# The last local-attention pair of an encoder kernel: V turned in one go, splits and Y's lower parts moved, a second weights buffer for the last merge

## The chip, the cores and the metric

One core of a Trainium2 chip runs the whole program. The metric is the time of one execution on the device, in microseconds (us); the kernel before and the changed kernel are compared by the median of several executions.

## The reference, cut to what matters

A two-layer encoder trunk on one sequence of 1,024 tokens by 1,024 features, float32.

```
x = x + even_mixer(rmsnorm(x))     # 8 heads dilated windows (mixer A), 8 heads 2-D neighbourhood (mixer B)
x = x + swiglu(rmsnorm(x))
x = x + odd_mixer(rmsnorm(x))      # differential attention, 8 heads
x = x + swiglu(rmsnorm(x))
out = rmsnorm(x)

# even_mixer
proj = h @ w_in                                       # q, k, v of both mixers
ya = dilated_mixture_attention(qa, ka, va)            # branches weighted by their softmax denominators
yb = neighborhood_attention(qb, kb, vb, rpb)          # each token: 8 x 16 neighbours on a 16 x 64 grid
y = concatenate([ya, yb]) @ w_out
```

## The kernel before, in words

**Pairs.** Attention works on pairs of heads P: 0 to 3 are mixer A, 4 to 7 mixer B ("local"), 8 to 15 the second layer. The change touches the end of mixer B, pair 7, and the output projection behind it (`out_projection(0)`). Each pair has eight steps n, one for 128 queries (for a local pair, a stripe of 8 grid columns), and each step handles both heads m = 0 and 1.

**Precision.** Every product is made of three passes: an operand x is split into a high part (ScalarE rounds it, `ACT.Copy` to fp32r) and a lower part (VectorE subtracts the high part from x). So each tile of weights (`w_split`, WR to WS), each turned tile of probabilities (`hi`, `lo`, to ATB), each block of V (`vhi`, `vlo`, to VS) and each block of the attention output Y (`y_high`, `y_low`, to HH and HL) costs a ScalarE and a VectorE instruction, the second waiting for the first.

**One step of a local pair.** TensorE computes scores (`qk`, L2462) one step ahead; VectorE adds the bias table and takes the minimum (`ttr`, L1760); ScalarE takes the exponential with the row sum (`exp`, L1141); TensorE transposes the probabilities (`turn`, L2501); ScalarE and VectorE make high and lower part (`hi` L1182, `lo` L1835). After each second step TensorE multiplies with V (`pv`, L2545), ScalarE copies one half (`y_copy`, L1231) and VectorE adds the other (`y_add`, L1844).

**The order of the work.** Each engine's program is a list written out by hand (`attention_mixed` once for each engine), with waits on semaphores between engines; each engine works strictly in its list's order. Tables say at which step something is put in: `splits(P)` (weight splits, as step: strip ahead, slot, fills that must be done), `turned_v` (the transposes of V, `tv`, L2395), `Y_AT` and `Y_LOW_AT` (high and lower parts of Y), `Y_ORDER` (the order in which blocks of Y go into the projection). In pairs 4 to 6 the next pair's projection (`fill`, L2381) fills TensorE between the steps. In pair 7 nothing is left to fill with behind step 0, where its own V is finished.

**V in pair 7.** The second half of V is evacuated by VectorE at step 1 (`evac`, L1715). The transposes of V come in two batches of four: the first between the two turns of step 1, the second behind them.

**The output projection.** `op_item(0, i)` multiplies block `Y_ORDER[0][i]` of Y with two strips of `w_out` (12 matmuls of 512 columns). It waits for i + 1 lower parts of Y. Item 0 stands between the two turns of step 7; items 1 and 2 stand behind the last turn, each followed by one of the last two products with V; item 3 and the spread of the row sums follow, then the rest:

```
for m in range(2):
    op_item(0, m + 1)
    pv(7, NQ - 1, m)
op_item(0, 3)
```

**The merge of mixer A.** The three dilated branches are kept as two partial outputs and merged for each pair: MY = MY x weight 0 (`merge_start`), MZ = MZ x weight 1, MY += MZ (`merge_rest`), all on GpSimd, in chunks of 256 columns, four instructions for each. Both weights are broadcast from DRAM into one buffer, MA, so the second weights are fetched only when the first multiplication is done. The result goes to `y_dram` and is loaded back as a block of Y (YE for blocks 0 and 1, Y for the others); `y_scale` multiplies blocks 4 to 6 with their reciprocal row sums on GpSimd. Pair 3's merge runs beside pair 7.

**Transfers.** All loads named here are issued by SyncE in the order of `attention` and `out_projection` in `sync_program`. `raw(w)` loads the two halves of weight strip w into WR, each once the split of the strip before has freed it.

## Time and profile before

| | us |
|---|---|
| median of 3 runs | 2536.59 |
| lowest, highest | 2532.62, 2537.97 |
| the profiled execution's own time | 2532.99 |
| its span (first to last instruction) | 2531.0 |
| mean granted TensorE clock in it | 0.997 of full |
| TensorE busy | 2502.5 |
| VectorE busy | 1758.6 |
| ScalarE busy | 1155.8 |
| GpSimd busy | 413.7 |

The profile records one execution. PE is TensorE, DVE VectorE, ACT ScalarE, POOL GpSimd, SP SyncE. A busy time is the sum over an engine's instructions; in a timeline, an instruction's idle time before it is given in brackets with what ended it. Matmuls are pipelined, so rows overlap; the step between two starts is the time one costs. The granted clock is given as a share of 2.4 GHz. Pair 7 lies from about 470 us to 500 us.

### The profile page before, as it was taken

The numbers are of one execution on the slowest core, as the hardware profiler recorded it, in microseconds if no ns is written. First come the engines' busy times: TensorE is split into PE (matmuls) and PEld (weight loads), VectorE is DVE, ScalarE is ACT, GpSimd is POOL, SyncE is SP. The second block draws the span as 40 slices with busy tenths as digits, with TensorE's granted clock in tenths as the row PEclk, the third lists the DMA queues.
The fourth block names the chain that finished last, engine by engine and source line by source line (L and its number), as shares of the span: only waits on it lengthen the run. The fifth ranks groups of instructions, "written<-read, shape, count | busy, mean of one in ns | idle before, by whom it ended". The sixth has DMA issues, their size and how long they took to land.

```text
span 2531.0 us, 34993 instructions
## 1 busy us (share of the span) xinstructions
PE 2502.5 (99%) x12931; PEld 2065.0 (82%) x12931; DVE 1758.6 (69%) x2647; ACT 1155.8 (46%) x2016; POOL 413.7 (16%) x320
## 2 busy tenths in 40 slices
PE   9999999899999999999999999999999999999998
PEld 7888777688888888888888888888888888888887
DVE  6556565656878878666577777777657878887654
ACT  6555554625333333444455455556343333334434
POOL 1001022400332333100000000000002333232001
PEclk9999999999999999999999999999999999999999
DMA  3222253633444444866211111111334444447764
GB/s 130 61 60 74 53 134 94 186 127 117 147 178 162 146 171 166 316 216 210 80 48 50 50 50 50 48 49 71 117 108 143 168 155 164 156 154 268 237 194 145
DMA packets 189171, 332.38 MB, mean 131 GB/s; under 512 B 59728, under 2 KB 67792, under 8 KB 180816
## 3 DMA queue, kind: packets, MB, share of 16 engines
q1 hardware_dynamic: 154208, 320.62, 37.5%
q10 hardware_dynamic: 34800, 9.60, 1.8%
q8 instruction: 101, 1.65, 0.3%
q14 instruction: 62, 0.51, 0.1%
HBM read 238.24 MB, written 91.91 MB: 130 GB/s over the span
## 4 chain that ended last, share of the span: by engine, by line
PE 93%; issue 2%; DVE 2%; ACT 1%; DMA 1%; SPq 1%; POOL 0%; ACTq 0%; POOLq 0%; DVEq 0%
PE PS L2381 20%; PE PS L2296 18%; PE PS L2297 18%; PE PS L2298 18%; PE PS L2545 4%; PE PS L2477 4%; PE PS L2501 3%; PE PS L2493 1%; PE PS L2448 1%; PE PS L2522 1%; PE PS L2395 1%; PE PS L2462 1%; PE PS L2304 1%; PE PS L2526 1%; PE PS L2438 0%
## 5 line engine op out<-in xcount | busy, mean ns | idle before, releaser
L2381 PE MATMUL PS<-HH,WS 128*128 128x512 f32 x1536 | 515.9, 402 | 3.5 <-DVE HL L1623 1.1
L2381 PEld LDWEIGHTS PS<-HH,WS 128*128 128x128 f32 x1536 | 285.5, 188 | 59.9 <-issue 1.6
L2381 PE MATMUL PS<-HL,WS 128*128 128x512 f32 x768 | 301.4, 393 | 0.0
L2097 DVE TENSOR_TENSOR SPLIT<-RAWI,SPLIT 128x1024 fp32r<-128x1024 f32 x154 | 194.2, 1265 | 149.9 <-ACT SPLIT L1450 149.9
L1450 ACT ACTIVATE SPLIT<-RAWI 128x1024 fp32r<-128x1024 f32 x154 | 162.9, 1060 | 205.7 <-PE PS L2298 152.2
L2296 PE MATMUL PS<-TH,WS 128*128 128x512 f32 x640 | 249.2, 389 | 2.3 <-ACT SIL L1442 2.3
L2298 PE MATMUL PS<-TH,WS 128*128 128x512 f32 x640 | 249.0, 389 | 0.0
L2297 PE MATMUL PS<-TL,WS 128*128 128x512 f32 x640 | 249.0, 389 | 0.0
L2296 PE MATMUL PS<-SPLIT 128*128 128x512 f32 x616 | 240.2, 390 | 0.0
L2298 PE MATMUL PS<-SPLIT 128*128 128x512 f32 x616 | 239.7, 389 | 0.0
L2297 PE MATMUL PS<-SPLIT 128*128 128x512 f32 x616 | 239.7, 389 | 0.0
L2296 PE MATMUL PS<-FH,WS 128*128 128x512 f32 x608 | 236.9, 390 | 0.0
L2298 PE MATMUL PS<-FH,WS 128*128 128x512 f32 x608 | 236.6, 389 | 0.0
L2297 PE MATMUL PS<-FL,WS 128*128 128x512 f32 x608 | 236.5, 389 | 0.0
L1424 ACT ACTIVATE WS<-WR 128x512 fp32r<-128x512 f32 x136 | 85.1, 629 | 242.0 <-PE PS L2298 116.6
L1760 DVE CUSTOM_DVE_ANT_0 PS<-PS,BIASC 128x1024 f32<-128x1024 f32 x128 | 154.2, 1246 | 24.4 <-PE PS L2477 23.3
L2381 PEld LDWEIGHTS PS<-HL,WS 128*128 128x128 f32 x768 | 145.0, 189 | 25.2
L2041 DVE TENSOR_TENSOR WS<-WR,WS 128x512 fp32r<-128x512 f32 x136 | 118.3, 871 | 61.1 <-ACT WS L1424 61.1
L2041 DVE TENSOR_TENSOR WS<-UR,WS 128x512 fp32r<-128x512 f32 x120 | 106.0, 884 | 71.5 <-ACT WS L1424 71.3
L1424 ACT ACTIVATE WS<-UR 128x512 fp32r<-128x512 f32 x120 | 75.8, 632 | 153.5 <-PE PS L2298 113.7
L2296 PEld LDWEIGHTS PS<-TH,WS 128*128 128x128 f32 x640 | 120.1, 188 | 28.1 <-ACT SIL L1442 3.2
L1145 ACT ACTIVATE EC<-PS,ST 128x1024 f32<-128x1024 f32 x128 | 141.2, 1114 | 3.8 <-DVE ST L1760 3.8
(274 smaller groups left out, 4969.8 us busy)
## 6 DMA issues: line engine op xcount, KB each, us to landing
WR<-wstrips SPq DMA_DIRECT2D x224, 256.0 KB, 2.7
RAWI<-ab_scratch SPq DMA_DIRECT2D x154, 256.0 KB, 4.2
ab_scratch<-SIL SPq DMA_DIRECT2D x132, 256.0 KB, 2.0
WD<-wdown SPq DMA_DIRECT2D x22, 1024.0 KB, 7.5
wd_scratch<-WD SPq DMA_DIRECT2D x22, 1024.0 KB, 3.9
RAWI<-wd_scratch SPq DMA_DIRECT2D x88, 256.0 KB, 3.3
UR<-wstrips SPq DMA_DIRECT2D x80, 256.0 KB, 3.3
RAWI<-wdown SPq DMA_DIRECT2D x66, 256.0 KB, 3.8
```

Source lines behind the costliest of these rows:

```text
L1145: e.activation(e_tile(kind, m, n)[:, 0:128 * nk], banks(S_BANK[m], 2)[:, 0:128 * nk], ACT.Exp, scale=-1.0, bias=ST[:, n % 2, m:m + 1], acc ...
L1424: e.activation(WS[:, slot, 0, :], src, ACT.Copy).then_inc(S["w_hi"], 1)
L1450: e.activation(SPLIT[m % 6][:, 0], RAWI[:, m % 4], ACT.Copy).then_inc(S["ihi"], 1)
L1760: e.tensor_tensor_reduce(out=s, in0=s, in1=(table if kind == "C" else table[:, m, :])[:, c:c + 128 * nk], scale=-1.0 if kind == "B" else 1 ...
L2041: e.tensor_tensor(WS[:, slot, 1, :], src, f(WS[:, slot, 0, :]), ALU.subtract).then_inc(S["w_lo"], 1)
L2097: e.tensor_tensor(SPLIT[m % 6][:, 1], RAWI[:, m % 4], f(SPLIT[m % 6][:, 0]), ALU.subtract).then_inc(S["ilo"], 1)
L2296: e.matmul(ps, wh, xh, start=start, stop=False, skip_group_check=on)
L2297: e.matmul(ps, wh, xl, start=False, stop=False, skip_group_check=on)
L2298: return e.matmul(ps, wl, xh, start=False, stop=stop, skip_group_check=on)
L2381: last = e.matmul(ps, wt, xt, start=g == 0, stop=g == 23)
L2477: last = e.matmul(PS[:, S_BANK[m] + c // 4, 0:wd], QS[r, a, q], KS[r, P % 2, b, k], start=i == 0, stop=i == 2)
L2545: last = e.matmul(PS[:, bank, lo_:hi_], v, p, start=i == 0, stop=i == len(todo) - 1)
```

## The change

- **V in one go.** Both batches of V's transposes stand between the two turns of step 1, and ScalarE's two high parts of V stand ahead of the exponentials of step 2.
- **Splits.** The two `w_out` strips are split at the ends of steps 2 and 4 of pair 7, not at the end of step 0 and the beginning of step 6.
- **Lower parts of Y.** They stood at steps 3, 5 and 7 (one, one, two), ahead of the step's second lower part of ATB. Now one stands at step 5 and one at step 7, each behind it, and the next two behind the loop. Blocks 5 and 3 exchange their places in `Y_ORDER`.
- **The last merge.** A second buffer, MB, takes the weights 1 of pair 3, in the place of QS2 (free once the scores of pair 6 are done). `merge_last` issues the transfers in another order: MA, MZ, MY, MB.
- **SyncE.** The load of the second `w_out` strip moves from the end of `attention` to a place behind the loads of Y and behind `merge_store(3)`; the load of block 3 of Y and the row sums of block 6 follow it.

```diff
--- before.py
+++ after.py
@@ -148,6 +148,9 @@
     assert place[0] <= nc.sbuf_usable_end
     place[0] = mixed + 2 * 5 * 2 * 256 * 4
     QS2 = sb("QS2", [128, 2, T], f32r)
+    place[0] = mixed + 2 * 5 * 2 * 256 * 4
+    MB = sb("MB", [128, T])
+    place[0] = mixed + 2 * 5 * 2 * 256 * 4 + 2 * T * 4
     MY = sb("MY", [128, T])
     MZ = sb("MZ", [128, T])
     MA = sb("MA", [128, T])
@@ -492,7 +495,7 @@
             return {1: (4, P % 2, 6), 3: (5, 1 - P % 2, 8), 5: (6, P % 2, 10)}
         if kind_of(P) == "B":
             slot = strip_of(P, 0) % 2
-            return {0: (3, 0, 4)} if P == 7 else {0: (3, 1 - slot, 4), 1: (4, slot, 6), 4: (5, 1 - slot, 8)}
+            return {2: (3, 0, 4), 4: (4, 1, 6)} if P == 7 else {0: (3, 1 - slot, 4), 1: (4, slot, 6), 4: (5, 1 - slot, 8)}
         if P == 15:
             return {1: (3, 0, 5), 3: (4, 1, 6)}
         if P == 3:
@@ -504,6 +507,8 @@
         if P == 0 and n < 2:
             return ([(0, 0), (0, 1)], [(0, 2), (0, 3)]) if n == 0 else ([(0, 4), (1, 0)], [(1, 1)])
         if 3 <= P < 8:
+            if P == 7:
+                return ([(P, 0), (P, 1)], []) if n == 1 else ([], [])
             return ([(P, 0)], [(P, 1)]) if late(P) and n == 1 else ([], [])
         if late(P):
             first, second = {0: ([], [0]), 1: ([1], [])}.get(n, ([], []))
@@ -512,9 +517,9 @@
         return [(P + 1, b) for b in first], [(P + 1, b) for b in second]
 
     Y_AT = {2: 0, 3: 1, 4: 2, 5: 3, 6: 4, 7: 5}
-    Y_LOW_AT = {3: [0], 5: [1], 7: [2, 3]}
+    Y_LOW_AT = {5: [0], 7: [1]}
     SQUARED_AT = {2: [0, 1], 3: [2], 4: [3, 4], 5: [5, 6]}
-    Y_ORDER = [[0, 1, 2, 4, 3, 5, 6, 7], list(range(KC))]
+    Y_ORDER = [[0, 1, 2, 4, 5, 3, 6, 7], list(range(KC))]
 
     def at_slots(P, n, m, kind, half):
 
@@ -619,6 +624,19 @@
             e.wait_ge(S["a_out"], 16 * (P + 1))
             merge_weights(P, 0)
             e.dma_start(MZ[:, :], ya_dram[P, 1]).then_inc(S["mgz_full"], 16)
+
+        def merge_last():
+
+            e.wait_ge(S["mg_done"], 12 * 3)
+            e.wait_ge(S["a_out"], 16 * 4)
+            merge_weights(3, 0)
+            e.dma_start(MZ[:, :], ya_dram[3, 1]).then_inc(S["mgz_full"], 16)
+            e.wait_ge(S["ym_out"], 16 * 3)
+            e.dma_start(MY[:, :], ya_dram[3, 0]).then_inc(S["mgy_full"], 16)
+            e.wait_ge(S["qk_done"], 8 * 7)
+            for m in range(2):
+                e.dma_start(MB[64 * m:64 * m + 64, :],
+                            a_dram[3, 1, m].partition_broadcast(64)).then_inc(S["mgz_full"], 16)
 
         def merge_second(P):
             e.wait_ge(S["mg_done"], 12 * P + 4)
@@ -663,16 +681,17 @@
                 if 4 <= P < 7:
                     merge_store(P - 4)
                 if P == 6:
-                    merge_first(3)
+                    for m in range(2):
+                        e.wait_ge(S[f"y_out{m}"], 1 + 64 * 4)
+                    merge_last()
                     e.wait_ge(S["pv_done"], 2 + unit(6, NQ - 1, 1, "B") + 1)
                     for k in range(2):
                         merged_load(k)
-            raw(W_OUT[layer] + 1, layer)
+            if layer:
+                raw(W_OUT[1] + 1, 1)
 
         def out_projection(o):
 
-            if o == 0:
-                merge_second(3)
             e.wait_ge(S["fill_done"], 48 * (o + 1))
             if o == 0:
                 merged_load(2)
@@ -686,10 +705,11 @@
                 for m in range(2):
                     e.wait_ge(S[f"y_out{m}"], 1 + 16 * 28)
                 e.dma_start(Y[:, 6, :], y_dram[6]).then_inc(S["yl_full6"], 16)
+                merge_store(3)
+                raw(W_OUT[0] + 1, 0)
+                merged_load(3)
                 e.wait_ge(S["rows_out"], 96)
                 spread_sums(6)
-                merge_store(3)
-                merged_load(3)
             else:
                 for m in range(2):
                     e.wait_ge(S[f"y_out{m}"], 1 + 16 * 42)
@@ -933,11 +953,14 @@
         def merge_rest(P):
 
             w = T // 4
-            e.wait_ge(S["mgz_full"], 16 * (P + 1))
-            e.wait_ge(S["mga_full"], 64 * P + 64)
+            if P == 3:
+                e.wait_ge(S["mgz_full"], 16 * 4 + 32)
+            else:
+                e.wait_ge(S["mgz_full"], 16 * (P + 1))
+                e.wait_ge(S["mga_full"], 64 * P + 64)
             for r in range(NCLS):
                 z = MZ[:, w * r:w * r + w]
-                e.tensor_tensor(z, z, MA[:, r:T:NCLS], ALU.mult).then_inc(S["mg_done"], 1)
+                e.tensor_tensor(z, z, (MB if P == 3 else MA)[:, r:T:NCLS], ALU.mult).then_inc(S["mg_done"], 1)
             for r in range(NCLS):
                 e.wait_ge(S["mg_done"], 12 * P + 5 + r)
                 y = MY[:, r:T:NCLS]
@@ -1312,8 +1335,6 @@
                     kq_high(*v)
                 if n == 7 and 1 <= P <= 4:
                     weights_exp(P - 1)
-                if P == 7 and n == 6:
-                    w_split(w + 4, 1, 0, ("fill_done", 6 * P + 6))
                 if last:
                     y_copy(*last, 0, kind_of(last[0]))
                 hi(P, n, 0, kind)
@@ -1325,13 +1346,17 @@
                 for v in middle(P, n):
                     if v[1] >= 2 and late_scores:
                         kq_high(*v)
+                if P == 7:
+                    for v in first:
+                        vhi(*v)
                 if after:
                     exp(*after, 0, kind_of(after[0]))
                 for v in middle(P, n):
                     if v[1] >= 2 and not late_scores:
                         kq_high(*v)
-                for v in first:
-                    vhi(*v)
+                if P < 7:
+                    for v in first:
+                        vhi(*v)
                 if after and (kind == "A" or P == 7):
                     exp(*after, 1, kind_of(after[0]))
                 if last:
@@ -1903,8 +1928,6 @@
                 for m in range(2):
                     if after:
                         ttr(*after, m)
-                if P == 7 and n == 6:
-                    w_split(w + 4, 1)
                 if last:
                     y_add(*last, 0)
                 if n < NQ - 1:
@@ -1914,9 +1937,6 @@
                         evac(*v)
                 if kind == "B" and n == NQ - 1:
                     lo(P, n, 0, kind)
-                if P == 7:
-                    for i in Y_LOW_AT.get(n, []):
-                        y_low(0, Y_ORDER[0][i], i)
                 for v in first:
                     vlo(*v)
                 if last:
@@ -1927,6 +1947,9 @@
                     evac(P + 1, 0)
                 if not lower_later(P, n):
                     lo(P, n, 1, kind)
+                if P == 7:
+                    for i in Y_LOW_AT.get(n, []):
+                        y_low(0, Y_ORDER[0][i], i)
                 for v in second:
                     vlo(*v)
                 if n in splits(P):
@@ -1935,11 +1958,13 @@
                     weights_first(P - 1)
                 if n == NQ - 1 and P >= 4:
                     recip(P)
+            y_low(0, Y_ORDER[0][2], 2)
+            y_low(0, Y_ORDER[0][3], 3)
+            y_add(7, NQ - 1, 0)
             y_low(0, Y_ORDER[0][4], 4)
-            y_add(7, NQ - 1, 0)
-            y_low(0, Y_ORDER[0][5], 5)
             y_add(7, NQ - 1, 1)
-            y_low(0, Y_ORDER[0][6], 6)
+            for i in (5, 6):
+                y_low(0, Y_ORDER[0][i], i)
 
         def attention_diff():
             begin(1)
```

In the program's order this looks so on VectorE. **Step 1 of pair 7**, from the split of `w_out` (WS<-WR) over the evacuation of V (FS<-PS,RSTD) and the adds of the scores (ISA) to V's lower parts (VS). Before:

```order
L1601 TENSOR_TENSOR WS<-WR,WS 128x512 [waits w_hi] x2
L1715 TENSOR_TENSOR FS<-PS,RSTD 128x8x8x8 [waits kq_lo,fill_done]
L1760 ISA PS,ST<-PS,BIAS_80 128x384 [waits qk_done]
L1760 ISA ST 128x1
L1760 ISA PS,ST<-PS,BIAS_80 128x384 [waits qk_done]
L1760 ISA ST 128x1
L1835 TENSOR_TENSOR ATB<-PS,ATB 128x3x128 [waits hi_done]
L1738 TENSOR_TENSOR VS<-PS,VS 128x8x64 [waits vhi_done]
L1835 TENSOR_TENSOR ATB<-PS,ATB 128x3x128 [waits hi_done]
L1738 TENSOR_TENSOR VS<-PS,VS 128x8x64 [waits vhi_done]
```

Now:

```order
L1740 TENSOR_TENSOR FS<-PS,RSTD 128x8x8x8 [waits kq_lo,fill_done]
L1785 ISA PS,ST<-PS,BIAS_80 128x384 [waits qk_done]
L1785 ISA ST 128x1
L1785 ISA PS,ST<-PS,BIAS_80 128x384 [waits qk_done]
L1785 ISA ST 128x1
L1860 TENSOR_TENSOR ATB<-PS,ATB 128x3x128 [waits hi_done]
L1763 TENSOR_TENSOR VS<-PS,VS 128x8x64 [waits vhi_done] x2
L1860 TENSOR_TENSOR ATB<-PS,ATB 128x3x128 [waits hi_done]
```

The split is gone from in front of the evacuation, and both lower parts of V stand together, ahead of the step's second lower part of ATB.

**End of step 2 of pair 7**, from the sum of Y (Y<-PS,YS) to the first add of the scores of step 4. Before:

```order
L1844 TENSOR_TENSOR Y<-PS,YS 64x2x16x8 [waits y_copy]
L1835 TENSOR_TENSOR ATB<-PS,ATB 128x3x128 [waits hi_done]
L1844 TENSOR_TENSOR Y<-PS,YS 64x2x16x8 [waits y_copy]
L1835 TENSOR_TENSOR ATB<-PS,ATB 128x3x128 [waits hi_done]
L1760 ISA PS,ST<-PS,BIAS_80 128x384 [waits qk_done]
```

Now:

```order
L1869 TENSOR_TENSOR Y<-PS,YS 64x2x16x8 [waits y_copy]
L1860 TENSOR_TENSOR ATB<-PS,ATB 128x3x128 [waits hi_done]
L1869 TENSOR_TENSOR Y<-PS,YS 64x2x16x8 [waits y_copy]
L1860 TENSOR_TENSOR ATB<-PS,ATB 128x3x128 [waits hi_done]
L1626 TENSOR_TENSOR WS<-WR,WS 128x512 [waits w_hi] x2
L1785 ISA PS,ST<-PS,BIAS_80 128x384 [waits qk_done]
```

The split of `w_out` stands between the step's last lower part and the next add. At the end of step 4 the same is found again.

**Step 7 of pair 7**, from the lower part of the first turn, over Y's lower parts (HL), to the reciprocal of the row sums. Before:

```order
L1835 TENSOR_TENSOR ATB<-PS,ATB 128x2x128 [waits hi_done]
L1982 TENSOR_TENSOR HL<-Y,HH 128x1024 [waits yhi_done] x2
L1835 TENSOR_TENSOR ATB<-PS,ATB 128x2x128 [waits hi_done]
L1788 RECIPROCAL LR<-LS 128x16 [waits exp_done]
L1792 COPY BIAS_79<-LR 128x1024 [waits rec_done]
L1982 TENSOR_TENSOR HL<-Y,HH 128x1024 [waits yhi_done]
```

Now:

```order
L1860 TENSOR_TENSOR ATB<-PS,ATB 128x2x128 [waits hi_done] x2
L2007 TENSOR_TENSOR HL<-YE,HH 128x1024 [waits yhi_done]
L1813 RECIPROCAL LR<-LS 128x16 [waits exp_done]
L1817 COPY BIAS_79<-LR 128x1024 [waits rec_done]
L2007 TENSOR_TENSOR HL<-Y,HH 128x1024 [waits yhi_done] x2
L1869 TENSOR_TENSOR Y<-PS,YS 64x2x16x8 [waits y_copy]
L2007 TENSOR_TENSOR HL<-Y,HH 128x1024 [waits yhi_done]
```

One of Y's lower parts (HL<-YE, the second in number) stands behind the lower part of the last turn; the third and fourth, which stood ahead of it, come behind the reciprocal.

## Rows read from the trace of the kernel before

**Rows 1.** The page's part 1, busy time by engine.

```profile
PE 2502.5 (99%) x12931; PEld 2065.0 (82%) x12931; DVE 1758.6 (69%) x2647; ACT 1155.8 (46%) x2016; POOL 413.7 (16%) x320
```

**Rows 2.** Windows of 10 us: busy, clock, DMA share, GB/s.

```profile
core 0: us, PE busy (x) PEld busy (x) DVE busy (x) ACT busy (x) POOL busy (x), PEclk, DMA share, GB/s
470.00:480.00 10.00, 6.21 (x45) 4.95 (x44) 7.86 (x17) 5.93 (x15) 3.53 (x5) 0.94 1.04 304
480.00:490.00 10.00, 7.59 (x52) 5.57 (x51) 7.76 (x18) 8.92 (x22) 10.00 (x10) 0.89 0.85 235
490.00:500.00 10.00, 9.03 (x42) 7.21 (x43) 7.32 (x17) 7.52 (x19) 4.96 (x3) 0.66 0.52 159
```

**Rows 3.** Timeline of PE: start us, us, instruction, [idle before <-releaser].

```profile
470.84 0.55 PE L2501 MATMUL PS<-IDENT,E 128*128 128x128 f32 x3
473.44 0.65 PE L2395 MATMUL PS<-IDENT,FS 128*128 128x128 f32 x4 [2.05 <-DVE FS L1715]
...
477.32 0.92 PE L2545 MATMUL PS<-ATB,VS 128*128 128x256 f32 x6 [1.74 <-DVE VS L1738]
...
496.87 0.77 PE L2296 MATMUL PS<-HH,WS 128*128 128x512 f32 x1
...
500.79 0.38 PE L2501 MATMUL PS<-IDENT,E 128*128 128x128 f32 x2
500.93 0.48 PE L2296 MATMUL PS<-HH,WS 128*128 128x512 f32 x1
...
503.77 0.81 PE L2545 MATMUL PS<-ATB,VS 128*128 128x256 f32 x6
```

**Rows 4.** Timeline of DVE, same columns.

```profile
470.87 1.91 DVE L1601 TENSOR_TENSOR WS<-WR,WS 128x512 fp32r<-128x512 f32 x2 [1.02 <-ACT WS L1036]
472.71 0.68 DVE L1715 TENSOR_TENSOR FS<-PS,RSTD 128x512 f32<-128x512 f32 x1
...
476.58 0.69 DVE L1738 TENSOR_TENSOR VS<-PS,VS 128x512 fp32r<-128x512 f32 x1
...
489.78 0.56 DVE L1760 CUSTOM_DVE_ANT_0 PS<-PS,BIAS 128x384 f32<-128x384 f32 x1
...
491.24 1.91 DVE L1982 TENSOR_TENSOR HL<-YE,HH 128x1024 fp32r<-128x1024 f32 x1
...
494.26 1.28 DVE L1601 TENSOR_TENSOR WS<-WR,WS 128x512 fp32r<-128x512 f32 x2
...
495.80 0.54 DVE L1835 TENSOR_TENSOR ATB<-PS,ATB 128x384 fp32r<-128x384 f32 x1
...
500.60 0.42 DVE L1835 TENSOR_TENSOR ATB<-PS,ATB 128x256 fp32r<-128x256 f32 x1 [3.16 <-ACT ATB L1182]
...
504.43 1.22 DVE L1982 TENSOR_TENSOR HL<-Y,HH 128x1024 fp32r<-128x1024 f32 x1
```

**Rows 5.** Timeline of ACT, same columns.

```profile
474.52 0.59 ACT L1175 ACTIVATE VS<-PS 128x512 fp32r<-128x512 f32 x1
...
492.92 1.17 ACT L1036 ACTIVATE WS<-WR 128x512 fp32r<-128x512 f32 x2
...
499.23 1.06 ACT L1287 ACTIVATE HH<-Y 128x1024 fp32r<-128x1024 f32 x1 [2.39 <-DMA Y<-y_scratch]
...
501.21 0.39 ACT L1182 ACTIVATE ATB<-PS 128x256 fp32r<-128x256 f32 x1 [0.65 <-PE PS L2501]
```

**Rows 6.** Windows of 1 us, PE alone: busy, clock, DMA share, GB/s.

```profile
472.00:473.00 1.00, 0.00 (x0) 1.00 0.98 372
480.00:481.00 1.00, 1.00 (x8) 0.50 1.01 410
```

**Rows 7.** Timeline of POOL, same columns as rows 3.

```profile
479.84 3.33 POOL L940 TENSOR_TENSOR MZ<-MZ,MA 128x256 f32<-128x256 f32 x4 [6.47 <-DMA MA<-a_scratch]
483.12 4.30 POOL L944 TENSOR_TENSOR MY<-MY,MZ 128x256 f32<-128x256 f32 x4
```

**Rows 8.** DMA issues 455 to 500 us, then line L570, 400 to 540 us.

```profile
WR<-wstrips SPq DMA_DIRECT2D x2, 256.0 KB, 4.1
...
DMA to landing us min/median/max: 2.6/3.2/11.0
```


## The prediction

> **What bounds the kernel now.** TensorE is busy in 99% of the span [rows 1], so only what opens, closes or slows a hole on TensorE moves the end. The views were read in this order: the engines' shares, then TensorE's waits by size, then windows of 10 us around the place that the diff touches. Nearly everywhere TensorE is full; the stretch of the last local pair (P = 7, from 470 to 500 us) is not. TensorE is busy 6.21, 7.59 and 9.03 us of each 10, and part of that at the lower clock: 0.94, 0.89 and 0.66 of full [rows 2]. The idle time there is 7.2 us; at the 1.2 GHz level (half) it spent 2 x (0.06 + 0.11) x 10 = 3.4 us and then 2 x 0.34 x 10 = 6.8 us. That is all there is to win. ScalarE is busy 8.92 us and VectorE 7.76 us of the middle 10 [rows 2]: the loop score, add-and-minimum, exponential, turn, high, low, product goes round through both. From 496.87 on, when the output projection's first item starts, TensorE has no hole for the rest of the projection. So the change is worth what it shifts that start, plus what it does behind it.
>
> **Part 1, V in one go and the split out of its way (n = 0 and 1): opens the stretch earlier.** In the kernel before, both V transposes wait for VectorE. The evacuation of V's second half stands behind a weight split: the split runs 470.87 to 472.71 (1.91 us for the two), the evacuation 472.71 to 473.40 [rows 4], and the transposes start at 473.44 after a wait of 2.05 [rows 3]. Then the product of n = 1 waits 1.74 more, until 477.32, for V's last lower part, which runs at 476.58 [rows 3, 4]. Now the evacuation is the first thing after the fill, so it runs from 470.9 - 0.6 = 470.3 to 470.95. The transposes follow the turn of 470.84 (step about 0.3) at 471.15 and stand together, 0.5 each. V's two high parts (0.59 each [rows 5]) start at 471.8, the last lower part (0.69) ends at 473.7, and the product can start at 473.8: **3.5 us earlier** than 477.32. ScalarE's copy of that product moves as much.
>
> **Part 2, the two splits put into the loop at n = 2 and n = 4: takes most of it back.** The splits are not gone, they are moved. The first cost the front 1.91 on VectorE; the second stood at n = 6 (1.17 on ScalarE [rows 5], 1.28 on VectorE [rows 4]). Their new place is behind ScalarE's high part of Y (1.06 for one [rows 5]). VectorE finishes its lower part, waits for that and for the first half of the split (1.0 + 0.6), then works 1.28 (1.91 where GpSimd is busy), and only behind it comes the add-and-minimum of the next scores, for which the next exponential waits. Against the old order, where the add followed the lower part at once, the shift falls at each split. From 3.5 it goes to about 2.4 at n = 3: ScalarE itself has 1.17 more to do, while VectorE's share hides behind the row sums that ScalarE copies and sends there, ahead of its exponential. Through n = 4 it stays near 2.5. The add-and-minimum that began at 489.78 [rows 4], right behind the lower part, could so begin at 487.3; with 1.0 of waiting and 1.28 of the second split ahead of it, it begins at about 489.5: **0.3 us of shift is left**.
>
> **Part 3, the lower parts of Y out of the middle: gives some back.** At n = 3 that lower part cost nothing (ScalarE was later than it). At n = 5 it ran 1.91 at 491.24 [rows 4] and held the lower part behind it by about 0.95; the split at n = 6 (until 495.47) held Y's sum and the lower part at 495.80 [rows 4] by as much again. One lower part of Y (1.22 to 1.91) now stands at the end of n = 5 instead. Net 1.9 - 1.2 = 0.7. The first projection item, at 496.87 [rows 3], so starts 0.3 + 0.7 = **1.0 us earlier** (0.7 to 3.4: the upper end is part 1 without part 2).
>
> **Part 4, the second lower part of Y behind the last turn: a new wait.** Item 1 of the projection needs two lower parts of Y. In the kernel before, the second was made at n = 5. Now it is at n = 7 and behind the lower part of the last turn, and TensorE issues that turn only between item 0 and item 1. Counted from the old times: turn at 500.79 [rows 3], its high part from 501.21 to 501.60 [rows 5], its lower part 0.42 as the row of 500.60 [rows 4], to 502.02; then Y's lower part, 1.22 with GpSimd quiet [rows 4], to 503.2. TensorE was ready for item 1 at 500.93 [rows 3]: it waits **2.3 us** (2.0 to 3.0, the upper end with the 1.91 that a lower part took beside a busy GpSimd). Nothing can cover this, since everything else that TensorE has left is queued behind item 1. Items 2 to 7 find their lower parts ready: a reciprocal and a copy (0.9 together, about) and one lower part (1.2) end 2.1 us behind it, and item 2 starts only after the 2.8 us of item 1 and a product.
>
> **Part 5, the merge and the queue: nothing on the path.** In the kernel before, ScalarE waited 2.39 us for the merged Y of the last mixer-A pair [rows 5], at 499.23, while TensorE was full: it cost nothing, and its going gives nothing. The second weights buffer lets GpSimd's second step, which waited 6.47 us for its weights and ran at 479.84, with the adds behind it to 487.4 [rows 7], end at about 479. The exchange of two items, 5 and 3, puts the reuse of the weight slot one item later (2.8 us); its next use is over 6 us off. So 0 for all of it, unless a transfer comes late (below).
>
> **Part 6, the clock behind the new wait.** At 480 us the granted clock was 0.50 [rows 6], 2.5 us after the wait that ended at 477.32; yet at 472 us, in a microsecond without any TensorE work, it was 1.00 [rows 6]. A fall costs dense work dearly. Item 0 took 500.79 - 496.87 = 3.92 us, partly at half clock, item 1 503.77 - 500.93 = 2.84 [rows 3]: 1.1 lost. Ends: nothing, or a fall as the first one (3.4 us), which costs 1.7 in full work. I take the fall, because the new wait of 2.3 us stands closer to sparse work and is longer than either of the two at the front. The Trainium skill (TensorE: Matmul & The Clock Gate, "The HAM clock gate") has the clock fall only behind an idle stretch; by that rule a short wait with full work on both sides costs no clock, and the sum would be 1.3. Behind that rule stands the 472 us row; the fall at 478.8 (0.06 x 2 x 10 = 1.2 us before 480 [rows 2]), in the midst of work, is against taking it so strictly.
>
> **Sum.** -1.0 + 2.3 + 1.7 = +3.0 us on the profiled execution (2532.99). It stands 3.6 below the median of the three runs, which spread over 5.4 us. On the median, 2536.6 + 3.0 = **2539.6**.
>
> **Rivals.**
> - *No fall of the clock* behind the new wait: +1.3, so 2537.9. For it: the microsecond at 472 us, after which the clock stayed. Chance 0.28. The Trainium skill's clock page, named above, stands on this side.
> - *Part 1's shift survives and the pair's end gets denser.* 3.4 us stay, and the 6.8 us at half clock do not come, which saves item 0's 1.1: -3.4 - 1.1 + 2.3 = -2.2, so 2534.4. For it: ScalarE and VectorE both have holes of about 1 us in the loop. Against: the split waits for ScalarE's high part each time. Chance 0.14.
> - *Slower: the weights of the second strip come late.* Their load stood in front of the Y loads and was issued long before use. Now SyncE issues it behind all of them, behind the store of the merged Y, and behind the first split (about 480), and ScalarE wants it at 487.6, with exponentials queued behind. In that stretch such a load took 4.1 us, but the longest took 11.0 [rows 8]. At 11.0 it lands at 491.5, and all waits 3.9: 3.0 + 3.9 = 6.9, so 2543.5. It decides once the load takes over 7.6 us, and crosses 0.2% at 9.7. The DMA engines were busy 1.04 and 0.85 of the time from 470 to 490 [rows 2], so it is not remote. Chance 0.10.
>
> **How the numbers follow.** Likeliest 0.45, the rivals 0.28, 0.14 and 0.10, 0.03 for what I don't see. 0.2% is 5.1 us, about what a measurement of this kernel can tell from no change. By mechanism only the last rival passes it, on the slow side; three runs of one kernel spread as wide as this, so a median adds some 2 us of its own. Slower 0.16 (0.10 and 0.06 of the likeliest), faster 0.08 (part of the second rival and chance), same 0.76. The range, 2533.0 to 2543.5, runs from a little below the fast case to the slow one.
>
> **What would show it.** Right: transposes of V with no wait at 471, the product of n = 1 near 473.8; VectorE waiting for ScalarE before both splits; the first item near 495.9; a TensorE wait of 2.0 to 3.0 us for VectorE's HL in front of the second item, and a clock of 0.50 in the microseconds behind it. Wrong: no such wait; a first item before 494.5; a ScalarE wait for WR at n = 4; or new waits beyond 530 us, where I expect none.

## The result, and the profile after

| | before | changed |
|---|---|---|
| median (6 runs each) | 2536.51 us | 2546.16 us |
| lowest, highest | 2532.0, 2537.97 | 2543.51, 2547.79 |
| ratio to before, 95% interval | | 1.0038 [1.0029, 1.0048] |
| the profiled execution | 2532.99 | 2546.15 |

The change costs 9.65 us of median, 0.38%. The prediction was 2539.6, range 2533.0 to 2543.5, with 0.16 for "slower by over 0.2%". The time lies outside the range.

First the page of the changed kernel (its span, and the busy time of each engine with its share of the span):

```profile
span 2544.0 us, 34992 instructions
PE 2505.4 (98%) x12931; PEld 2067.6 (81%) x12931; DVE 1761.6 (69%) x2647; ACT 1155.3 (45%) x2016; POOL 412.9 (16%) x320
```

TensorE does the same work (2505.4 us busy against 2502.5 [rows 1]) in a span that is 13.0 longer. The loss arises in pair 7 and the items behind it: from the end of pair 7's last fill (470.20 before, 470.36 now) to the spread of the row sums behind item 3 it was 40.5 us and is 54.6, 14.1 more, of which about 1 comes back in the rest of the program. The windows of 10 us there (columns as in rows 2) show TensorE at a third of its time from 480 to 490 and the clock near half for 20 us:

```profile
470.00:480.00 10.00, 6.72 (x52) 4.98 (x50) 5.14 (x14) 3.03 (x8) 8.71 (x12) 1.00 1.06 322
480.00:490.00 10.00, 3.38 (x13) 1.91 (x13) 3.85 (x6) 5.38 (x13) 5.26 (x3) 0.55 0.68 176
490.00:500.00 10.00, 7.53 (x40) 6.41 (x40) 6.42 (x16) 7.79 (x18) 1.66 (x1) 0.60 0.58 167
500.00:510.00 10.00, 6.59 (x32) 6.33 (x33) 7.49 (x17) 6.42 (x16) 0.84 (x2) 0.66 0.01 2
510.00:520.00 10.00, 7.94 (x32) 6.41 (x31) 5.84 (x9) 2.67 (x5) 0.00 (x0) 0.83 0.76 290
```

TensorE's timeline says where:

```profile
471.39 1.04 PE L2420 MATMUL PS<-IDENT,FS 128*128 128x128 f32 x8
...
474.00 0.92 PE L2570 MATMUL PS<-ATB,VS 128*128 128x256 f32 x6 [0.53 <-DVE VS L1763]
...
482.07 0.88 PE L2526 MATMUL PS<-IDENT,E 128*128 128x128 f32 x3 [4.83 <-DVE ATB L1860]
486.63 0.37 PE L2442 MATMUL PS<-IDENT,LR 128*16 128x128 f32 x1 [3.69 <-issue]
...
491.81 1.94 PE L2570 MATMUL PS<-ATB,VS 128*128 128x256 f32 x8 [2.34 <-DVE ATB L1860]
...
503.41 1.94 PE L2570 MATMUL PS<-ATB,VS 128*128 128x256 f32 x8 [4.07 <-issue]
...
508.30 0.48 PE L2321 MATMUL PS<-HH,WS 128*128 128x512 f32 x1
...
511.13 0.38 PE L2526 MATMUL PS<-IDENT,E 128*128 128x128 f32 x2
513.57 0.50 PE L2321 MATMUL PS<-HH,WS 128*128 128x512 f32 x1 [2.06 <-DVE HL L2007]
...
517.60 1.22 PE L2570 MATMUL PS<-ATB,VS 128*128 128x256 f32 x6
```

The transposes come without a wait (2.05 before [rows 3]), and the product of step 1 starts at 474.00 instead of 477.32. Then come two waits that the prediction does not have, 4.83 and 3.69 us, two more at 491.81 and 503.41 (2.34, 4.07), and the forecast one in front of item 1 (2.06). Item 0 starts 11.4 us later than in rows 3, not 1.0 earlier. VectorE, named as releaser of the first, was itself waiting; ScalarE's timeline has the origin:

```profile
480.44 0.38 ACT L1254 ACTIVATE YS<-PS 64x256 f32<-64x256 f32 x1 [5.83 <-DMA y_scratch<-YS]
...
485.70 0.38 ACT L1254 ACTIVATE YS<-PS 64x256 f32<-64x256 f32 x1 [3.24 <-DMA y_scratch<-YS]
...
502.42 0.58 ACT L1164 ACTIVATE E<-PS,ST 128x384 f32<-128x384 f32 x1 [2.85 <-DVE ST L1785]
```

ScalarE's first two copies of pair 7 (`y_copy`, L1254) wait 5.83 and 3.24 us for a DMA, y_scratch<-YS: the stores of pair 6's last products. `y_copy` writes YS, from which those stores read, so it waits for them to land. They were issued at 469.0 and 469.6, as before. Here are these two stores alone (tile YS, 468 to 500 us), of the changed kernel and then of the kernel before; the last line gives the shortest, the median and the longest of the two landing times:

```profile
L1279 ACTq DMA_DIRECT2D y_scratch<-YS x2: 533/588/643, 469.0 to 469.6; - x2
...
DMA to landing us min/median/max: 11.3/13.7/16.0
```

```profile
L1256 ACTq DMA_DIRECT2D y_scratch<-YS x2: 532/584/637, 468.9 to 469.5; - x2
...
DMA to landing us min/median/max: 5.3/5.6/5.8
```

The stores took 5.3 and 5.8 us and now take 11.3 and 16.0. 469.0 + 11.3 is 480.3 and 469.6 + 16.0 is 485.6, where the two waits end. In the kernel before they had landed at about 474.2 and 475.3, and ScalarE's two copies came at 478.28 and 480.33, so with 4.1 and 5.0 us to spare. The first of these copies there waited for TensorE:

```profile
478.28 0.38 ACT L1231 ACTIVATE YS<-PS 64x256 f32<-64x256 f32 x1 [1.73 <-PE PS L2545]
```

Next to the late stores stands SyncE:

```profile
470.39 0.32 SPq L647 DMA_DIRECT2D Y<-y_scratch  x1
470.80 0.94 SPq L701 DMA_DIRECT2D Y<-y_scratch  x2
471.80 2.39 SPq L593 DMA_DIRECT2D YQ<-l_scratch  x4
485.68 0.33 SPq L707 DMA_DIRECT2D Y<-y_scratch  x1
...
489.52 0.93 SPq L575 DMA_DIRECT2D WR<-wstrips  x2
```

The loads of Y and of the row sums now go out in one run from 470.39, right behind the two stores. In the kernel before, SyncE had other things to wait for and they went out from 474.59 on:

```profile
474.59 0.53 SPq L629 DMA_DIRECT2D Y<-y_scratch  x1
```

The load of block 6, which also waits for the stores, is issued at 485.68 and confirms the landing. VectorE and GpSimd explain the two later waits. The second fence is line L1626 alone, first from 486 to 491 us and then from 497 to 503, durations in ns as least/median/most, then the first and the last start:

```profile
488.10 2.00 DVE L1626 TENSOR_TENSOR WS<-WR,WS 128x512 fp32r<-128x512 f32 x2 [0.91 <-ACT WS L1059]
...
498.69 3.15 DVE L1626 TENSOR_TENSOR WS<-WR,WS 128x512 fp32r<-128x512 f32 x2 [0.91 <-ACT WS L1059]
501.77 0.55 DVE L1785 CUSTOM_DVE_ANT_0 PS<-PS,BIAS 128x384 f32<-128x384 f32 x1
...
512.30 1.21 DVE L2007 TENSOR_TENSOR HL<-YE,HH 128x1024 fp32r<-128x1024 f32 x1
```

```profile
L1626 DVE TENSOR_TENSOR WS<-WR,WS x2: 680/1040/1400, 488.1 to 489.4; 128x512 fp32r<-128x512 f32 x2
L1626 DVE TENSOR_TENSOR WS<-WR,WS x2: 679/1614/2548, 498.7 to 501.2; 128x512 fp32r<-128x512 f32 x2
```

```profile
484.27 4.67 POOL L996 TENSOR_TENSOR Y<-Y,YQ 128x1024 f32<-128x1024 f32 x2 [3.68 <-DMA YQ<-l_scratch]
498.34 2.35 POOL L996 TENSOR_TENSOR Y<-Y,YQ 128x1024 f32<-128x1024 f32 x1 [9.40 <-DMA YQ<-l_scratch]
```

Both splits hold the add-and-minimum behind them, and with it ScalarE's exponential (2.85 us at 502.42). The first takes 2.00 us and the second 3.15, where the second took 1.28 in its old place [rows 4]. In each split the first of the two halves is the long one: 1.40 us from 488.10 and 2.55 us from 498.69, the other 0.68. Each long half ends some 0.55 us behind the end of a GpSimd multiplication of 1,024 columns (488.94 and 500.69). The Trainium skill (SBUF — State Buffer, "Who interferes with whom") says that a VectorE instruction with two SBUF inputs contends with a GpSimd instruction that reads SBUF, over a pair of ports that works as an exclusive lock. These rows agree: the half lasts until GpSimd's instruction is over. Shorter GpSimd instructions cost VectorE something too. In the kernel before, the first split took 1.91 us [rows 4] beside instructions of 256 columns:

```profile
469.68 3.70 POOL L931 TENSOR_TENSOR MY<-MY,MA 128x256 f32<-128x256 f32 x4 [8.88 <-DMA MA<-a_scratch]
```

### The profile page after: what moved, and what is told of

Its sections match the earlier page's. It is cut to its first block, busy times and chain, and to the rows that moved or that the text cites. A ratio compares the mean times of both kernels' runs of the same rounds, so it can differ in the third digit from the quotient of the medians.

```text
span 2544.0 us, 34992 instructions
## 1 busy us (share of the span) xinstructions
PE 2505.4 (98%) x12931; PEld 2067.6 (81%) x12931; DVE 1761.6 (69%) x2647; ACT 1155.3 (45%) x2016; POOL 412.9 (16%) x320
## 4 chain that ended last, share of the span: by engine, by line
PE 94%; issue 2%; DVE 2%; DMA 1%; ACT 1%; SPq 0%; POOL 0%; ACTq 0%; POOLq 0%; DVEq 0%
PE PS L2406 20%; PE PS L2321 18%; PE PS L2322 18%; PE PS L2323 18%; PE PS L2570 5%; PE PS L2502 4%; PE PS L2526 3%; PE PS L2518 1%; PE PS L2473 1%; PE PS L2547 1%; PE PS L2329 1%; PE PS L2420 1%; PE PS L2487 1%; DMA y_scratch<-YS 1%; PE PS L2551 1%
```

## The experiments

**Theory A** is the first half of the above: the loads moved forward hold up the stores of pair 6, and ScalarE waits for these. Its rivals are B, the new places of the splits, and C, the orders of V and of Y's lower parts.

Each kernel was timed in alternation with the kernel before. "Over before" is the difference of the two medians, and the ratio with its interval decides (it is not the quotient of the two medians: for best_nobuf that is 0.9995). Single executions of the kernel before ranged from 2530.4 to 2542.3 in one series.

| run | over before, us | ratio, 95% interval |
|---|---|---|
| changed kernel | +9.65 | 1.0038 [1.0029, 1.0048] |
| after_again | +13.0 | 1.0048 [1.0035, 1.0062] |
| a_hold | +6.1 | 1.0021 [1.0012, 1.003] |
| a_buf | +4.4 | 1.0017 [1.0008, 1.0027] |
| b_merge | +3.6 | 1.0011 [1.0002, 1.0021] |
| a_buf_low1 | +2.4 | 1.0009 [1.0, 1.0018] |
| a_buf_spl | +1.2 | 1.0005 [0.9996, 1.0014] |
| b_buf | 0.0 | 1.0 [0.9991, 1.0009] |
| a_all | -2.2 | 0.9992 [0.9983, 1.0001] |
| best_nobuf | -1.3 | 0.9989 [0.998, 0.9998] |
| best | -3.0 | 0.9989 [0.998, 0.9998] |
| best2 | -2.3 | 0.9987 [0.9978, 0.9996] |

**a_buf: the changed kernel with the wait for the stores taken away.** A copy of mixer B fills 256 of YS's 512 columns, so pair 7 can use the others.

```diff
-            e.wait_ge(S[f"y_out{m}"], 1 + 64 * P + 16 * (n // 2 if P < 7 else 0))
+            e.wait_ge(S[f"y_out{m}"], 1 + 64 * P + 16 * (n // 2) if P < 7 else 1 + 64 * 4)
-                e.activation(pair_rows(YS[0:64, m, 0:w]), ...
+                e.activation(pair_rows(YS[0:64, m, y_at(P):y_at(P) + w]), ...
```

> The changed kernel, with ScalarE's copy of pair 7 going to columns 256 to 511 of YS (pairs 4 to 6 use 0 to 255), so that it no longer waits for the stores of pair 6 to land. Theory A (those stores lie in the DMA engines behind the loads of Y that SyncE now issues at 470.4 us instead of from 474.6 us, and ScalarE stands 5.83 and 3.24 us for them): ScalarE's first copy at about 475 us, no wait for y_scratch<-YS, first projection item 9 us earlier than in the changed kernel (508.3), 2537 us, no slower than the kernel before by more than 2 us. Theory B (the splits at the ends of steps 2 and 4, with VectorE behind ScalarE and beside GpSimd, make the loss): the first item no more than 3 us earlier, 2543 us or more. Theory C (V's order or the new place of Y's second lower part): under 3 us of gain too.

Its ratio is 1.0017 against 1.0038. The stores still take 10.7 and 14.6 us, but nobody waits for them. ScalarE's first copy starts at 475.14 behind TensorE, and no wait for y_scratch<-YS is left:

```profile
475.14 0.38 ACT L1257 ACTIVATE YS<-PS 64x256 f32<-64x256 f32 x1 [0.34 <-PE PS L2573]
...
482.15 0.58 ACT L1167 ACTIVATE E<-PS,ST 128x384 f32<-128x384 f32 x1 [1.53 <-DVE ST L1788]
...
490.39 1.17 ACT L1062 ACTIVATE WS<-WR 128x512 fp32r<-128x512 f32 x2 [0.95 <-DMA WR<-wstrips]
```

Item 0 starts at 498.15, 10.2 us before that of the changed kernel. So theory A holds for the larger half of the loss: 5.3 of 9.65 us, between two series. But 4.4 us over the kernel before are left, not 2; these three waits of TensorE remain:

```profile
483.29 1.94 PE L2573 MATMUL PS<-ATB,VS 128*128 128x256 f32 x8 [3.20 <-DVE ATB L1863]
...
493.91 1.48 PE L2573 MATMUL PS<-ATB,VS 128*128 128x256 f32 x8 [3.61 <-issue]
...
503.44 0.50 PE L2324 MATMUL PS<-HH,WS 128*128 128x512 f32 x1 [2.06 <-DVE HL L2010]
```

A part of the forecast for theory A was too simple: with the stores' wait gone, ScalarE now meets one for WR, 0.95 us (the last row of its fence above). It is the transfer that I had as the slow rival. In the changed kernel ScalarE has no wait for it. The two splits take 1.97 and 1.29 us on VectorE here.

**a_hold: the same wait kept, the traffic held back.**

```diff
+                for m in range(2):
+                    e.wait_ge(S[f"y_out{m}"], 1 + 16 * 28)
                 merged_load(2)
```

> The changed kernel, with SyncE holding the loads of Y blocks 2, 4 and 5 and of the row sums until the stores of pair 6 have landed; the wait of ScalarE stays. Theory A: without that traffic the stores land by about 474 to 476 us, ScalarE's first copy waits under 1.5 us, and the time is within 3 us of the run with its own columns (about 2538 us), unless the loads, now issued later, make ScalarE wait for YE or Y. Theory B or C: as slow as the changed kernel (2546). A variant of A, that the loads of YE and of the merge (issued before the stores) already hold the stores up: a wait of 4 us or more is left.

```profile
478.03 0.38 ACT L1256 ACTIVATE YS<-PS 64x256 f32<-64x256 f32 x1 [1.30 <-DMA y_scratch<-YS]
...
493.83 1.20 ACT L1061 ACTIVATE WS<-WR 128x512 fp32r<-128x512 f32 x2 [2.02 <-DMA WR<-wstrips]
```

Both stores now take 6.8 us, ScalarE's wait falls to 1.30, and the second one is gone. So it is the traffic that holds the stores up. They land at 478, not at 474 to 476, because they are issued 2.1 us later: in this execution the last fill already ends at 472.47, for a reason outside the edit. The price comes at the other end: WR's load is 2.02 us late. All in all 6.1 us over before.

**b_merge: the transfers alone, in the kernel before.** MB, `merge_last` and SyncE's order are taken from the change, nothing else.

> The kernel before with only the merge and SyncE's order of the change (MB, the new order of the last merge's transfers, the load of the second output strip behind the Y loads); V, splits and lower parts of Y as before. Theory A: this part alone brings the wait: the Y loads go out at 470.4 us, the stores land at 480 to 486 us, ScalarE's first copy of pair 7 (478.3 us before) waits 2 us and the second 3 to 5 us, the time is 2541 to 2544. Theory B or C: same as before, 2536.5.

```profile
480.46 0.38 ACT L1252 ACTIVATE YS<-PS 64x256 f32<-64x256 f32 x1 [3.61 <-DMA y_scratch<-YS]
...
485.15 0.38 ACT L1252 ACTIVATE YS<-PS 64x256 f32<-64x256 f32 x1 [2.66 <-DMA y_scratch<-YS]
```

The two waits, 3.61 and 2.66 us, appear without any of the other edits, and the stores take 11.1 and 15.2 us. So the moved transfers alone make the wait. The cost, 3.6 us, is under the 4.5 to 7.5 that I expected.

**b_buf: own columns in the kernel before.**

> The kernel before, with the same own columns for pair 7. In its profiled execution ScalarE waited for TensorE there, not for the stores, and that execution (2532.99) was 3.5 us under the median. Theory A with chance in it (the stores land late in some executions of the kernel before too): the runs gather near 2532 to 2533 and the median falls by 2 to 4 us. Without that: the same as the kernel before, 2536.5, within 1 us.

No change (1.0), and the stores take 5.3 and 5.4 us. The wait costs the kernel before nothing, and does not make the spread of its executions; where that comes from isn't settled. In this profile the stretch from the last fill to the spread of the row sums is 39.7 us, against 40.5, so one profile cannot show a difference of under 1 us there.

**a_buf_low1: Y's second lower part ahead of the last turn's.**

```diff
+                if P == 7 and n == NQ - 1:
+                    y_low(0, Y_ORDER[0][1], 1)
                 if not lower_later(P, n):
                     lo(P, n, 1, kind)
```

(and no longer behind it).

> The changed kernel with own columns of YS for pair 7, and the second lower part of Y at step 7 ahead of the last turn's lower part, not behind it. If my reading of that place is right, TensorE's wait of 2.06 us in front of the second projection item goes, and with it the fall of the clock behind it (item 1 takes 2.8 us, not 4.0): 3 us less than with own columns alone (2539.2 beside a kernel before of 2534.8), so some 1.5 us above the kernel before. If the wait only turns into another: no gain.

```profile
504.47 0.50 PE L2326 MATMUL PS<-HH,WS 128*128 128x512 f32 x1 [0.21 <-DVE HL L2012]
```

TensorE's wait in front of item 1 goes from 2.06 to 0.21 us. Item 1 and the product behind it are reached in 2.88 us, as at full clock, instead of 4.24 in a_buf. That is 3.2 us of the stretch. The time gained only 2 us (1.0009 against 1.0017, from two series). In this profile WR was 2.73 us late and the first split took 2.49.

**a_buf_spl: both splits back at their old places.**

> The changed kernel with own columns of YS for pair 7, and both splits of the output weights back at the end of step 0 and the beginning of step 6. Theory B' (with the wait for the stores gone, what the splits' new places cost is the next largest term): the waits of TensorE of 3.2 and 3.6 us at 483 and 494 us go, one of 2.0 us at 473 comes back, the first item starts 3 us earlier (about 496.5), 2536 us beside a kernel before of 2535. If the splits are not the cause of those two waits, they stay and the front's 2 us make it slower still: 2541.

TensorE's two waits at 483 and 494 us shrink to 0.33 and 0.34, and one of 1.43 us for the evacuation comes back. Item 0 starts 25.0 us behind the last fill, instead of 27.6. The time is 1.2 us over before, as expected. TensorE's wait in front of item 1 is here too:

```profile
502.43 0.50 PE L2328 MATMUL PS<-HH,WS 128*128 128x512 f32 x1 [2.06 <-DVE HL L2014]
...
505.29 0.81 PE L2577 MATMUL PS<-ATB,VS 128*128 128x256 f32 x6
```

Item 1 takes 2.86 us behind it, at full clock (a granted clock of 1.00 from 500 to 510 us). So the same 2.06 us were followed by a fall of the clock in the changed kernel (4.03 us for item 1), in after_again (4.43), a_buf and a_hold (4.24 each), but not here.

**a_all: the three together.**

> The changed kernel with all three named terms taken away together: own columns of YS, both splits at their old places, and the second lower part of Y ahead of the last turn's lower part. If these three are the whole loss, the time is that of the kernel before or 1 us less (what is left of the change is V in one go behind the old split, the merge and the block order): ratio 0.999 to 1.000. If something unnamed is left in the change: over 2 us above the kernel before.

0.9992: nothing is left of the loss. The three terms together are the whole of it. They do not add up exactly: one by one, over different series, they gave 5.3, 3.1 and 1.9 us; together it is 15.2 between this run and after_again, of the same series.

**best: what of the change is worth keeping.** The kernel before, with own columns and V in one go. The first split moves to pair 6, where TensorE is full of fills anyway:

```diff
+            if P == 6:
+                return {0: (3, 1 - slot, 4), 1: (4, slot, 6), 4: (5, 1 - slot, 8), 6: (6, 0, 10)}
-            return {0: (3, 0, 4)} if P == 7 else {...}
+            return {} if P == 7 else {...}
```

> The kernel before with own columns of YS for pair 7, V in one go, and the first output split moved to step 6 of pair 6, where the fills keep TensorE busy and its slot is free; second split, lower parts of Y, merge and SyncE's order as before. The front's shift of 3.5 us should then be kept, since nothing is added to the loop of pair 7: transposes at 471, product of step 1 near 474, the first item at about 493.5 instead of 496.9: 3.3 us under the kernel before, with no wait of ScalarE for y_scratch<-YS. The other way: pair 6 is full on VectorE there and TensorE waits in it, or the clock falls in the denser stretch: same as before.

```profile
474.52 0.92 PE L2556 MATMUL PS<-ATB,VS 128*128 128x256 f32 x6 [0.53 <-DVE VS L1749]
...
492.10 1.97 PE L2556 MATMUL PS<-ATB,VS 128*128 128x256 f32 x8 [2.29 <-DVE ATB L1846]
```

```profile
490.00:500.00 10.00, 6.72 (x22) 0.57 0.43 132
```

The front works as said: product of step 1 at 474.52, 3.6 us behind the last fill (7.1 before). It beats the kernel before, by 0.11% [0.02, 0.20]. In the profile none of the front's gain arrives, though. A product waits 2.29 us behind Y's lower part, and from 490 to 500 us the granted clock is 0.57 (the row above: TensorE's busy time, the clock, the DMA share, GB/s):

```profile
496.22 0.78 PE L2307 MATMUL PS<-HH,WS 128*128 128x512 f32 x1
...
501.68 0.48 PE L2307 MATMUL PS<-HH,WS 128*128 128x512 f32 x1
```

Item 0 starts 25.3 us behind the last fill (26.7 before), but item 1 only at 501.68: 5.5 us for item 0, against 3.9. To the spread of the row sums it is 40.5 us, as in the kernel before. That the 0.11% comes from the front is not shown.

**best_nobuf: the same, with the wait for the stores.**

> The same without own columns of YS, so with ScalarE's first copy of pair 7 waiting for the stores of pair 6. It comes some 3.5 us earlier than in the kernel before (474.9 us), while the stores landed in the kernel before at 478 to 479.6 us by SyncE's next issue. Theory A: ScalarE waits about 3 us for y_scratch<-YS and the front's gain is lost: equal to the kernel before within 1 us. If the stores have landed by 475 us, it equals the version with own columns.

```profile
477.44 0.38 ACT L1235 ACTIVATE YS<-PS 64x256 f32<-64x256 f32 x1 [2.39 <-DMA y_scratch<-YS]
```

The wait is there, 2.39 us. But the stores take longer here than in the kernel before, 7.9 and 8.3 us instead of 5.3 and 5.8. The kernel before did not hide a landing at 478: its stores were there by 475.3, and SyncE's next issue at 479.6, from which I took the landing, came late because SyncE was busy with other issues. With the first split in pair 6, SyncE issues the load of WR at 470.04, right behind the stores, instead of at 471.68, so this version moves a load, too. That this load is what slows the stores is argued, not tested. On the time the run does not decide: the ratio is that of best (0.9989), while the medians are 1.7 us apart and the stretch to the spread of the row sums is 41.8 us against 40.5.

**best2: blocks 5 and 3 exchanged, Y's second lower part at step 7.**

> The version of the run called best, with block 5 ahead of block 3 and the second lower part of Y moved from step 5 to step 7, ahead of the last turn's lower part. In that run's profile TensorE waits 2.29 us at 492.1 for a lower part that stands behind Y's, and ScalarE 6.14 us for block 3. Both should go; the projection's first item starts 1 to 2 us earlier: 4 to 5 us under the kernel before (ratio about 0.998). If the clock is what holds the stretch there (0.57 from 490 to 500 us), the gain is under 1 us more: ratio 0.9985 to 0.999.

0.9987, no different from best. The 2.29 and the 6.14 us are gone, but ScalarE now waits 2.85 us for GpSimd's multiplication of block 4, and the clock is 0.67 from 490 to 500. The second of the two outcomes.

**after_again: the changed kernel once more.**

> The changed kernel itself, on the same chip and beside the same runs of the kernel before as the two others: 1.003 to 1.005 of it, with ScalarE waiting for y_scratch<-YS again. If its wait was chance of one profile, the wait differs by more than half here.

1.0048, with waits of 5.07 and 3.00 us for y_scratch<-YS. The stores take 10.6 and 15.0 us. The wait is no chance of one profile.

## Why the prediction was wrong

**Part 1 (front): right.** The product came at 474.00; 473.8 was said.

**Part 5 (merge and queue, "nothing on the path"): wrong, and the step that failed.** I asked of every moved transfer who waits for it, and found nobody in need. I did not ask whom it delays. Loads issued 4 us earlier fell upon two stores issued 1 us before them, on whose landing ScalarE's next copy depended. That dependence is in the code (`y_copy` waits for `y_out`) but in no row of the trace before, since there the copies came 4.1 and 5.0 us after the landings. Part 5 moved the landings from 474.2 and 475.3 to 480.3 and 485.6, and does it alone, too (b_merge: waits of 3.61 and 2.66 us, 3.6 us in the median). Part 1 made it worse: it brought the copy forward by 3 us (475.14 in a_buf), to about where the stores used to land. a_buf prices the wait in the changed kernel: 5.3 us between the medians of the changed kernel and a_buf, each over its own runs of before.

**Part 2 (splits): direction right, size too small.** I had it take back 3.2 of the 3.5 us. With the stores' wait away (a_buf), item 0 stands 27.6 us behind the last fill, against 26.7 before: all of the 3.5 is gone and 0.9 more, of which 0.95 can be ScalarE's wait for WR. The splits' durations were as I had them there (1.97 and 1.29 us; 1.91 and 1.28 said). What the waits of 3.20 and 3.61 us of TensorE behind them are made of is not separated further; putting the splits back takes 2.6 us off the start of item 0 and 3.1 off the time (a_buf_spl, over two series). In the changed kernel itself the second split took 3.15 us, because the shift of 10 us put GpSimd's long multiplication beside it.

**Part 3 (-0.7): not measured** by itself; it is inside the 0.9.

**Part 4 (new wait): right.** 2.06 us; 2.3 was said. **Part 6 (clock): the size came as said, with some luck.** From item 1 to the product behind it it took 4.03 us instead of 2.84, and that product 1.05 instead of 0.65: 1.6 lost; 1.7 was said. The granted clock of 0.83 from 510 to 520 us makes 3.4 us at the 1.2 GHz level, the length I had taken. The fall began amid dense work, 1.5 us after the wait had ended. By the rule of the Trainium skill (TensorE: Matmul & The Clock Gate, "The HAM clock gate") such a wait costs nothing. In four runs it did cost something, and in a_buf_spl it did not, so my reason, the length of the wait, does not decide it.

**The rivals.** The slow one was a late transfer in the same crowd, and it is real (0.95, 2.02 and 2.73 us in a_buf, a_hold, a_buf_low1), but it was not the one that counted here. The chance for "slower" (0.16) rested mostly on it. Its 11.0 us, the longest load of [rows 8], came from the wider window of that row, 400 to 540 us; from 455 to 500 both loads of WR took 4.1 to 4.2. The 7.2 us idle and 10.2 at half clock bounded the gain. Nothing bounded the loss, and the upper end of the range rested on that one transfer.

## What to carry to other kernels

When a transfer is issued earlier, list what is in flight at its new time, and who waits for those: a wait on a buffer's release may be in the code and in no row, because something else was later, here by 4 us. The same holds when a step is made earlier: every semaphore it waits on gets a new chance to be the last. And work moved to another place meets other neighbours; its old duration was that of its old neighbours.

## What the runs showed of the hardware

- Two stores of 64 KB in pieces of 64 bytes, on ScalarE's queue, landed 5.3 and 5.8 us after issue in the kernel before (5.3 and 5.4 in b_buf), and 11.3 and 16.0 with 2.5 MB of loads issued on SyncE's queue right behind them (11.1 and 15.2 in b_merge, 10.6 and 15.0 in after_again). With these loads held back it was 6.8 (a_hold). Being issued first did not help. The Trainium skill (DMA: Bandwidth & Descriptors, "Queues, rings and completion order") says that each DMA engine takes turns between the queues packet by packet. The packets fit that: from 468 to 480 us in the kernel before, ScalarE's queue moved 0.13 MB in 2,080 packets, SyncE's 3.45 MB in 1,109, so a small piece may stand behind a large one each time. No run separates this from a mere lack of bandwidth.
- Half a split on VectorE, 0.68 us alone, took 2.55 beside one GpSimd multiplication of 2.35 us, and 1.40 beside the end of another. Beside GpSimd instructions of 256 columns (0.93 us each) a whole split took 1.91 instead of 1.28, at most 2.49 (a_buf_low1). No run changes the length of GpSimd's instructions alone.
- TensorE's clock: in the changed kernel it was at the 1.2 GHz level for 9.0 of the ten microseconds from 480, 8.0 from 490 and 6.8 from 500 (granted 0.55, 0.60, 0.66, each 2 x the missing share), though TensorE worked 7.53 us of the second ten. In best it stayed there through nearly all of item 0, 5.5 us without a gap. Behind one and the same wait of 2.06 us it fell in four runs and stayed at 2.4 GHz in a fifth (a_buf_spl).
